# Expert weights laid out with neighbouring rows on a partition, and w2 halved by rows, in a two-layer decoder trunk on one core

## The reference, cut to what matters

```python
hidden = silu(einsum('bsd,edf->bsef', h, w1)) * einsum('bsd,edf->bsef', h, w3)
hidden = hidden * gates[..., None]
return einsum('bsef,efd->bsd', hidden, w2)
```

## Time and profile before

| | |
|---|---|
| median of 3 runs | 1217.82 us (1216.81 to 1221.8) |
| profiled execution, its own time | 1216.76 us |
| its span, first to last instruction | 1215.0 us |
| mean granted TensorE clock | 0.969 |
| TensorE busy | 1150.2 us (95%) |
| VectorE, ScalarE, GpSimd busy | 431.4, 267.9, 93.5 us |
| read from memory | 307.55 MB |

### The profile page before, as it was taken

The page is one execution under the profiler, slowest core; times in us unless marked ns, Lnnn a source line. Parts: engine busy times, 40 slices in busy tenths (PEclk is TensorE's granted clock), DMA queues, the critical chain, the costliest instruction groups (busy, mean ns, idle before and its releaser), DMA issues.

```text
span 1215.0 us, 15687 instructions
## 1 busy us (share of the span) xinstructions
PE 1150.2 (95%) x6523; PEld 762.4 (63%) x6523; DVE 431.4 (36%) x946; ACT 267.9 (22%) x439; POOL 93.5 (8%) x106
## 2 busy tenths in 40 slices
PE   4799999998989999999999799979999999999997
PEld 2686698984478844444445478838887844444455
DVE  0364654265720321111111484874423411111113
ACT  2222010414220311111111353323331311111113
POOL 5002221200000100000000001331000100000000
PEclk9899899999989899999999899998988999999999
DMA  9797765329967379959999630000069689999991
GB/s 352 262 331 276 277 229 187 138 98 381 402 238 266 121 292 385 387 201 369 387 386 340 246 104 35 1 0 2 2 218 390 223 306 386 387 387 386 387 383 42
DMA packets 157180, 309.56 MB, mean 255 GB/s; under 512 B 9568, under 2 KB 10940, under 8 KB 157116
## 3 DMA queue, kind: packets, MB, share of 16 engines
q1 hardware_dynamic: 156320, 307.39, 69.5%
q10 hardware_dynamic: 796, 1.23, 0.3%
HBM read 307.55 MB, written 1.05 MB: 254 GB/s over the span
## 4 chain that ended last, share of the span: by engine, by line
PE 86%; DVE 6%; SPq 2%; ACT 2%; DMA 1%; issue 1%; ACTq 1%; DVEq 0%
PE bank L1136 19%; PE bank L779 15%; PE bank L1160 10%; PE bank L840 7%; PE bank L1069 6%; PE bank L1061 6%; PE bank L790 2%; PE bank L906 2%; DVE scratch L2406 2%; PE bank L812 1%; PE bank L749 1%; PE bank L1193 1%; PE bank L1201 1%; PE bank L1372 1%; DVE scratch L2408 1%
## 5 line engine op out<-in xcount | busy, mean ns | idle before, releaser
L779 PE MATMUL bank<-arena,ring 128*128 128x256 f32 x960 | 211.5, 382 | 5.5 <-DMA ring<-in_ev_w_in 2.8
L779 PEld LDWEIGHTS bank<-arena,ring 128*128 128x128 f32 x960 | 182.8, 191 | 30.8 <-DMA ring<-in_ev_w_in 3.2
L1136 PE MATMUL bank<-ring,arena 128*64 128x512 f32 x704 | 153.7, 592 | 0.0
L1136 PEld LDWEIGHTS bank<-ring,arena 128*64 128x64 f32 x704 | 50.4, 137 | 99.6 <-issue 99.4
L2280 DVE TENSOR_TENSOR arena<-arena,bank 128x512 f32<-128x512 f32 x17 | 11.7, 688 | 220.7 <-PE bank L1136 220.7
L840 PE MATMUL bank<-arena,ring 128*128 128x256 f32 x384 | 86.1, 388 | 2.8 <-DVE arena L2504 2.8
L1069 PE MATMUL bank<-arena 128*128 128x256 f32 x336 | 83.1, 394 | 1.7 <-issue 1.7
L1136 PE MATMUL bank<-arena 128*64 128x512 f32 x384 | 84.1, 592 | 0.0
L840 PEld LDWEIGHTS bank<-arena,ring 128*128 128x128 f32 x384 | 74.8, 195 | 14.0 <-issue 3.2
L1061 PEld LDWEIGHTS bank<-arena 128*128 128x128 f32 x608 | 69.3, 192 | 13.8 <-issue 13.8
L1061 PE MATMUL bank<-arena 128*128 128x128 f32 x608 | 72.7, 278 | 0.0
(11 more groups left out here) (358 smaller groups left out, 1337.4 us busy)
## 6 DMA issues: line engine op xcount, KB each, us to landing
ring<-in_moe_w SPq DMA_DIRECT2D x112, 1024.0 KB, 14.2
arena<-in_moe_w SPq DMA_DIRECT2D x80, 1024.0 KB, 14.2
ring<-in_mod_w SPq DMA_DIRECT2D x24, 2048.0 KB, 11.0
ring<-in_ev_w_in SPq DMA_DIRECT2D x13, 2048.0 KB, 12.8
ring<-in_od_w_rkv SPq DMA_DIRECT2D x6, 2048.0 KB, 13.6
ring<-in_ev_w_out SPq DMA_DIRECT2D x4, 2048.0 KB, 17.1
ring<-in_od_w_o SPq DMA_DIRECT2D x2, 2048.0 KB, 10.7
arena<-in_x ACTq DMA_DIRECT2D x1, 1024.0 KB, 9.1
```

Source lines behind the costliest of these rows:

```text
L779: mm = pe.matmul(ps[:, c * S:(c + 1) * S], w_cols(slot)[:, k, (2 * half + c) * P:(2 * half + c + 1) * P], src[:, k, :], start=(k == 0), st ...
L1136: mm = pe.matmul(bank[4 + half][e * C:(e + 1) * C, :], hgT[:, kb, e * C:(e + 1) * C], piece(slots[e], kb), start=(kb == 0), stop=(kb == KB ...
```

## The change

1. **Which rows a partition holds.** A half of w1 or w3 puts rows 8p+4h to 8p+4h+3 on partition p: one run of 8 KB. A half of w2 is now rows 4p+2h and 4p+2h+1 with all 1024 columns: also one run of 8 KB.
2. **The operands follow.** A matmul contracts over the partition, so the tokens and the hidden product must be permuted alike. ScalarE writes `hN` with a stride (element 8p+k of a row goes to column 128k+p, L1688), and VectorE writes `hid` with a stride (element 4p+f goes to column 128f+p, L2280). Reads stay in order; consecutive writes are 512 bytes apart.
3. **w2 by row halves.** TensorE runs the 16 w2 matmuls as: rows half 0 into bank 5, then bank 6; rows half 1 into bank 5, then bank 6. Bank 5 is complete after 12 matmuls, not 8.
4. **Halves released on their own.** `w1_done` and `w3_done` count halves, `down_half` counts three steps for a block (rows half 0 used, bank 5 complete, all complete). SP waits for each half and refills it with two loads. Three matmuls of the first gather raise the counters by 1, 1 and 2, and all waits shift by that.

```diff
                         g_end = sp.value_load(tab_i[0:1, NE - 1:NE], min_val=1, max_val=NE)
-                        sp.wait_ge(M[l - 1]["w3_done"], g_end)
+                        sp.wait_ge(M[l - 1]["w3_done"], g_end * 2 + 1)
...
-                        sp.wait_ge(M[l - 1]["down_half"], g_end * 2)
+                        sp.wait_ge(M[l - 1]["down_half"], g_end * 3 + 2)
...
-                        sp.wait_ge(M[l - 1]["w1_done"], g_end)
+                        sp.wait_ge(M[l - 1]["w1_done"], g_end * 2 + 1)
...
                     pair, kind = divmod(d, 3)
-                    src = row_block(t[names[kind]][l, 2 * pair + e])
-                    src = src[:, :, h * W:(h + 1) * W] if kind == 2 else src[:, 4 * h:4 * h + 4, :]
-                    dst = weight_half(doubles[l][d][0][e], h).rearrange("p (k n) -> p k n", k=4)
+                    rows = 2 if kind == 2 else 4
+                    src = t[names[kind]][l, 2 * pair + e].rearrange("(p k) n -> p k n", p=P)[:, rows * h:rows * (h + 1), :]
+                    dst = weight_half(doubles[l][d][0][e], h).rearrange("p (k n) -> p k n", k=rows)
                     sp.dma_start(dst, src).then_inc(tile_landed[signal], 16)
...
-                def double_load(d):
-
-                    for h in range(2):
-                        for e in range(2):
-                            half_load(d, e, h, doubles[l][d][0][h])
+                def double_load(d, h):
+
+                    for e in range(2):
+                        half_load(d, e, h, doubles[l][d][0][h])
...
-                    if kind == 0:
-                        sp.wait_ge(base["w1_done"], done)
-                    elif kind == 1:
-                        sp.wait_ge(base["w3_done"], done)
-                    else:
-                        sp.wait_ge(base["down_half"], done * 2)
-                    double_load(d)
+                    for h in range(2):
+                        if kind == 2:
+                            sp.wait_ge(base["down_half"], done * 3 + 2 if h else done * 3)
+                        else:
+                            sp.wait_ge(base["w3_done" if kind else "w1_done"], done * 2 + 1 if h else done * 2)
+                        double_load(d, h)
...
-                def gather():
+                def gather(first=False):
...
                         if kb % 4 == 3:
                             mm.then_inc(m["gath_full"], 1)
+                        elif first and kb < 3:
+                            mm.then_inc(m[("w1_done", "w3_done", "down_half")[kb]], (1, 1, 2)[kb])
...
-                gather()
+                gather(first=True)
...
-                        mm.then_inc(m["w3_done" if half else "w1_done"], 1)
+                            if kb % 4 == 3:
+                                mm.then_inc(m["w3_done" if half else "w1_done"], 1)
...
-                    for half in range(2):
-                        if half:
-                            pe.wait_ge(m["hga_ready"], g + 2)
-                        slots = use(2, half)
-                        for f in range(FB):
-                            for e in range(2):
-                                mm = pe.matmul(bank[5 + half][e * C:(e + 1) * C, :], hidT[:, f, e * C:(e + 1) * C],
-                                               piece(slots[e], 4 * half + f), start=(f == 0), stop=(f == FB - 1))
-                        mm.then_inc(m["down_half"], 1)
+                    for rows in range(2):
+                        slots = use(2, rows)
+                        for half in range(2):
+                            if half and not rows:
+                                pe.wait_ge(m["hga_ready"], g + 2)
+                            for f in (2 * rows, 2 * rows + 1):
+                                for e in range(2):
+                                    v = f % 2 * D + half * W
+                                    mm = pe.matmul(bank[5 + half][e * C:(e + 1) * C, :], hidT[:, f, e * C:(e + 1) * C],
+                                                   weight_half(slots[e], rows)[:, v:v + W],
+                                                   start=(f == 0), stop=(f == FB - 1))
+                            if rows or half:
+                                mm.then_inc(m["down_half"], 1)
...
-                    act.activation(hN[:, tt, half * W:(half + 1) * W], bank[HN_BANK[u]][:], ACT.Copy).then_inc(m["hN_evac"], 1)
+                    by_row = hN[:, tt, :].rearrange("t (k p) -> t p k", k=KB)[:, half * HEAD:(half + 1) * HEAD, :]
+                    act.activation(by_row, bank[HN_BANK[u]][:].rearrange("t (p k) -> t p k", k=KB),
+                                   ACT.Copy).then_inc(m["hN_evac"], 1)
...
-                    act.wait_ge(m["w1_done"], g + 1)
+                    act.wait_ge(m["w1_done"], g * 2 + 3)
...
-                    act.wait_ge(m["down_half"], g * 2 + 1)
+                    act.wait_ge(m["down_half"], g * 3 + 4)
...
-                    dve.wait_ge(m["w3_done"], g + 1)
-                    tt_(hid, hsil, bank[5][:], ALU.mult).then_inc(m["hid_ready"], 1)
+                    dve.wait_ge(m["w3_done"], g * 2 + 3)
+                    tt_(hid.rearrange("s (f p) -> s p f", f=FB), hsil.rearrange("s (p f) -> s p f", f=FB),
+                        bank[5][:].rearrange("s (p f) -> s p f", f=FB), ALU.mult).then_inc(m["hid_ready"], 1)
...
-                    dve.wait_ge(m["down_half"], g * 2 + 2)
+                    dve.wait_ge(m["down_half"], g * 3 + 5)
```

## The result

The changed kernel takes 1225.01 us (median of 5 runs, 1222.71 to 1226.41); the kernel before, run beside it, 1216.81 us. The ratio is 1.006, 95% interval 1.0037 to 1.0083: 7.3 us slower, between 4.5 and 10.1. I had forecast 1219 us, no measurable change, and a range of 1215 to 1225, with 1.4 us for `hN` as the only cost in the sum. The loss is at that place, the one that I had called exposed, and it is larger than I had it: the median lies at the very end of the range. The profiled execution has a span of 1221.0 us, 6.0 more than before.

The account below looks back on a forecast made before the run. TensorE's own instructions were taken to bound the 17 blocks. Profiled 1216.76 us + 0 (loads, releases, w2, `hid`) + 1.4 (`hN`) = 1218.2, plus 1.06 to the median, 1219.2, stated as 1219 us; range 1215 to 1225.

Parts of the forecast that it names:

- the least that a measurement tells: Whole kernel: a measurement tells some 0.5%, 6.1 us, from no change; "same" ends at 1223.9 us.
- 5.3 us for changes of bank: w2 matmuls: two more bank changes at 0.31 us a block over 17 blocks; kept for the range, 0 in the sum.
- the dear end: `hN` copies: upper bound 8 x 0.34 = 2.7 us, from L2412, a VectorE block transpose writing with a 512-byte step.
- What bounds the kernel: The 17 expert blocks: TensorE's own instructions set their 28.41 us, loads have slack, 3.7 us at the tightest.
- Runs of 8 KB: Expert weight loads: rate stays or rises by some 6% (4 KB runs had 408 GB/s against 386); 0 us for TensorE.
- The rival in which the pattern costs rate: Expert loads: addresses 16 KB apart between partitions slow them; at 10% lower rate 15 us exposed, 1234 us; chance 0.06.
- Releases, signals: Expert loads: layer 1's start and land 3.4 us earlier, slack 3.7 to 7.1 us; added increments ride on matmuls; 0.
- w2 by row halves: w2 matmuls: same 16, bank 5 complete and its ScalarE copy 1.76 us later, 8 us to spare; taken as 0.
- Strided `hid`: VectorE's hidden product (L2280, 0.69 us): up to 0.34 us more, hidden, about 3 us needed to show; 0.
- Strided `hN`: ScalarE's four copies a layer (L1688), TensorE idle meanwhile: slowdown fully exposed, bounds 0 and 2.7 us, middle 1.4 taken.
- The cheap end, L2015: `hN` copies: lower bound 0, from a VectorE instruction writing with an 8-byte step at 1.18 ns an element.
- The clock: Rival: longer idle before L1104 halves the clock for slot matmuls and gather, 5.6 us a layer, 1231 us; chance 0.03.

Follow-up runs that it names:

- experiment 2: Changed kernel with `hN` and `hid` written in order, new loads, halved releases and w2 by row halves kept (another function): 1217.08 us, 0.9994 of the kernel before.
- experiment 6: Kernel before, `hN` copies writing with steps of 4 to 32 bytes in layer 0, 64 to 512 in layer 1, `hid` with 16 and 32: 1220.91 us, one run.
- experiment 1: Kernel before with only the strided write of `hN` added (another function): 1222.88 us, 1.0041 of the kernel before.
- experiment 4: Kernel before with three more in-order ScalarE copies among the four `hN` copies, late without a stride: 1220.97 us, 1.002 of the kernel before.

## Why the prediction was right or wrong, by its own steps

The forecast of no large change holds: the loss is 0.6%. But 7.3 us (4.5 to 10.1) is more than the 6.1 us that I had called the least that a measurement tells, and 1225.01 us is 6 us above the 1219 that I named. That the range reaches to it is luck. I had drawn its end from the dear copies and 5.3 us for changes of bank; the changes of bank cost nothing, and the loss came from copies dearer than the dear end and from a rival whose time, 1231 us, the range left out. Two of the bounds that I had named were crossed: four copies took 3.69 us where I had 3.4 at most, and the clock was below 1.00 at the first gather.

- **What bounds the kernel: right.** Blocks of 28.41 us at 322 and 420 GB/s, no wait of TensorE for a load of expert weights, and 0.9994 for all of the loads' edits by themselves (experiment 2).
- **Runs of 8 KB: right in effect, low in size.** I bounded the rate by the 4 KB runs' 408 GB/s; it came out at 420 to 423. The rival in which the pattern costs rate is dead.
- **Releases, signals: right at 0.** The loads of layer 1 ended some 13 us sooner, where I had expected 3 or more; most of that is the rate, which I had not put into their end.
- **w2 by row halves: right at 0.** 7.02 us a block as before, so three changes of bank cost no more than one and the 5.3 us that I kept for them was not needed. ScalarE's copy of bank 5 starts 485.24 - 479.89 = 5.35 us after w2's start in one block of layer 0; before it was 479.02 - 475.39 = 3.63, so 1.72 us later where I had 1.76.
- **Strided `hid`: right at 0.** 0.37 us more against my bound of 0.34, hidden with 3 us to spare.
- **Strided `hN`: this is the step that was wrong in size.** "With neither row close enough to decide I take the middle, 1.4 us" was a choice between 0 and 2.7 us; the copies cost 1.6 us a layer, 3.2 in all, above the dear end. The cheap end, L2015, was no evidence at all: its 8-byte step is on the free side of a limit at 16 bytes (experiment 6). L2412, with the step in question, was the row to go by, and it erred low by 0.14 us an instruction. The estimate from the Trainium skill's rule (experiment 6), 4 us, was too high by 0.8 us for the copies, the dear end, 2.7 us, too low by 0.5, and my 1.4 too low by 1.8.
- **The clock: a rival at 0.03 that came true, at a lower price.** I held against it that the idle was much shorter than the one before 694 us (7.1 us in the trace). But 1.97 us was enough in both layers of the changed kernel and of experiment 1, and 1.79 us in one of two (experiment 4). It was not enough every time: 1.97 us left the clock at 2.4 GHz in layer 1 of experiment 6. By the cases here (five of eight at such an idle) the chance, once the copies were slow, was about a half, neither 0.03 nor 1. The price was 1.6 us a layer, not 5.6, since the step set in some way into the slot matmuls and was over before the gather's end. With 3.2 us from the copies and 3.3 from the clock, the path behind the `hN` copies lost 6.5 us where I had 1.4, and that covers the measured 7.3 (4.5 to 10.1).
- **The chances.** Given that the copies slowed, the longer idle was sure, and the two costs are not independent: each slowing of the copies brings with it the chance of a clock step. I had priced them as if they were independent, the one in the sum and the other at 0.03.

## What to carry to other kernels

Before a permutation is put into an access pattern, look which side of which memory pays. On this kernel 16 bytes or more between neighbours in SBUF nearly doubled what a write by ScalarE takes, and 32 bytes between them doubled a gather whose weights TensorE loaded that way, while ScalarE's read of PSUM with a step of 32 bytes was free. When something is made later on the path of a busy TensorE, count the idle it makes twice: once as time, and once as what the granted clock may do to the matmuls behind it. Faster transfers behind a bound engine gave nothing that could be measured here, and the check for it is cheap: does a block's length depend on the GB/s beside it?

## What the runs showed of the hardware that I had not expected

- ScalarE writing 128x512 float32 to SBUF: 0.60 us with 4 or 8 bytes between neighbours, 1.05 to 1.15 us from 16 bytes up to 512, flat in between.
- TensorE's weight load of 128x128 float32 with a step of 32 bytes: 334 against 195 ns, and 4.05 us more on a gather of 3.77.
- Runs of 8 KB in place of 2 KB: 421 against 387 GB/s, 83453 packets against 157180.
- An idle of 1.75 to 1.97 us ahead of the slot matmuls was followed by a fall of the granted clock from 2.4 to 1.2 GHz in five of eight cases: both layers of the changed kernel and of experiment 1, and layer 0 of experiment 4. Layer 1 of experiment 4 (1.79 us) and both layers of experiment 6 (1.75 and 1.97 us) kept the clock. An idle of 0.8 us there kept it in all twelve cases. What decides between the five and the three stays open.
